# A two-layer hybrid trunk in split float32: small steps of mixers and cross attention between pieces of projections, final norm by tile

## The chip, the cores and the metric

The kernel runs on one core of one Trainium2 chip. The metric is device time in microseconds (us) of one execution, the median of the runs. PE is TensorE, DVE is VectorE, ACT is ScalarE, POOL is GpSimd, SP is SyncE, whose queue brings in the weights.

## What is computed

Two layers over x, 256 tokens of 1024 columns, in float32. In each layer:

```python
h = rms_norm(x, norm_mix[layer])
(aq, ak, av, bq, bk, bv, iq, ik, iw, cq, ckv, kr, gate_logits) = jnp.split(
    h @ w_in[layer], split_points, axis=-1)
o_a = window_gqa_sinks(...)      # 8 heads, window of 128, sinks, T5 bias
o_b = dsa_attention(...)         # token index scores, top 64 keys, 8 heads
o_c = mla_attention(...)         # low-rank q and kv, rotary keys, 8 heads
gates = jax.nn.sigmoid(gate_logits)            # three times 1024
merged = (gates[:, :, 0] * (o_a @ w_branch[layer, 0])
          + gates[:, :, 1] * (o_b @ w_branch[layer, 1])
          + gates[:, :, 2] * (o_c @ w_branch[layer, 2]))
x = x + merged @ w_out[layer]
hx = rms_norm(x, norm_xa[layer])
hm = rms_norm(mem, norm_mem[layer])
x = x + memory_cross_attention(hx, hm, xa_wq[layer], xa_wkv[layer], xa_wo[layer])
hf = rms_norm(x, norm_ffn[layer])
if layer % 2 == 0:
    x = x + swiglu(hf, ffn_w_gu[layer // 2], ffn_w_down[layer // 2])
else:
    x = x + moe_swiglu(...)      # router, 2 of 8 experts a token
```

and `rms_norm(x, final_norm)` at the end.

## The kernel before

**Weights.** All weights come from memory in units of 1 MB, by SP, into six slots of `raw`. A unit is cut into two pieces of up to 1024 columns. ACT copies a piece rounded into `whi` (L458), DVE subtracts that from `raw` and writes the rest into `wlo` (L461), both in the short float form `fp32r` that PE multiplies fast. `linear` multiplies each piece three times, high by high (L1500), activation low by weight high (L1506), activation high by weight low (L1514): 12 matmuls of up to 512 columns. There are four slots of pieces: the high half of piece p may be written once PE has used piece p - 4 (`piece_used`). The class `Splitter` does the splits in program order on ACT and on DVE; `through(l, name, b, ahead)` splits all up to the end of a block and `ahead` pieces more, `feed(n, ...)` splits n further ones. So ACT and DVE mostly have three or four pieces ready when they turn to other work.

**Blocks.** A layer has these projections, two blocks of up to 512 columns each: PA, PB, PC (inputs of the mixers A, B and C), GA, GB, GC (their gates), UQ and UKV (C's second projections), YA, YB, YC (the branches), WO (output), then XK, XQ, XV, XO (cross attention). The results of a block are in banks `lin_bank` = 2 * (number % 2) + t for the two tiles t of 128 tokens, so banks 0 to 3 alternate between blocks, and the small steps use banks 4 to 7. t = 0 sees 128 keys, t = 1 sees 256.

**Small steps.** `turn` transposes four 128-column stretches into a bank (L1527). TA, TB, TC, TQK, TM, TMEM, T2, TX, T3 are such transposes for q and k of each mixer, the merged branches, the memory and the norms. `scores` (L1549) multiplies q by k; DVE adds a bias and takes the maximum (L1845, L1848, L1855), ACT makes exponentials (L1296), DVE the inverse of the sum (L1873), POOL normalises (`normalise`, L1160). `attend` then turns the probabilities into `pT` and weighs v with them (L1568). B in addition has index products (L1624), ReLU on ACT, `index_scores` on DVE (L1934), the top-k (L1948 and L1950, eight rounds for 64 keys) and a mask that POOL adds (L1218).

**What sets the order.** It is written out by hand, one program for each engine; each engine works its list from the top, and waits on semaphores in it. On PE, each small step stands between two whole blocks, `attend` for both tiles in a row. All mixers share the two score tiles `sm` and one `pT`.

**Behind cross attention.** T3 transposes the sum x times the gain for the channel mixer. In layer 0 `dense_pe` first fills banks 4 to 7 by eight float32 matmuls with a cleared `scatter` (L644), then starts the first gate and up columns (L607, L608, L612). In layer 1 the router's weights are read by POOL once XO's last block has been added, DVE makes `r_lo`, PE multiplies the router (L1743), ACT and DVE rank the experts, tokens are gathered (L737), and a loop of eight trips runs the experts (`mixer_pe`, L785, L786, L791). A second pass, `experts2`, runs only if an expert has more than 128 tokens; the flag `more` says so, and here it does not run.

**The end.** Each engine reads `more`, branches, drains; then ACT squares x (`norm_sums`, L1262), DVE takes the mean (L1790), POOL the power (L1139), DVE multiplies (L1800), SP stores 1 MB (L1118).

Of the kernel before, what the change touches and what calls it, by code (L numbers as in the profile page):

```python
# [267 lines left out]
def trunk(nc, a, out, consts, onehot, known):  # L268
    with ExitStack() as ctx:
# [22 lines left out]
        h = place("h", [P, NT, D])  # L292
        biasA = place("biasA", [P, A_H, S])
# [15 lines left out]
        sm = [place("sm0", [P, 8, P], offset=region), place("sm1", [P, 8, S], offset=region + 4 * K1)]  # L309
        qC = place("qC", [P, NT, C_H, C_QK], offset=region)  # L310
        kC = place("kC", [P, NT, C_H, C_QK], offset=region + 6 * K1)
        pT = place("pT", [P, 2, 8, P], offset=region + 12 * K1)
# [19 lines left out]
        bias_vec = place("bias_vec", [16, 384], offset=region + 4 * K1)  # L332
        bias_rows = place("bias_rows", [P, 16, S], offset=region + 22 * K1)
# [78 lines left out]
        x_settled = sem("x_settled")  # L412

# [29 lines left out]
        class Splitter:  # L443
# [26 lines left out]

            def through(self, l, name, b, ahead=0):

                self.to(min(blocks[(l, name, b)].end + ahead, self.limit(l)))

# [24 lines left out]
        STAT_COLS = {"mix": (0, 2), "lora": (6, 4), "mem": (18, 2), "xa": (24, 2), "ffn": (30, 2), "fin": (72, 2)}  # L499
# [4 lines left out]

        def nkey(l, name):
            return ("fin",) if name == "fin" else (l, name)
# [17 lines left out]
        def prob_jobs(t, nk):  # L524
            return [(4 + 2 * kt + g, pT[:, kt, 4 * g:4 * g + 4, :], heads(bank[4 + 2 * kt + g][:, :], 4))
                    for kt in range(nk // P) for g in range(2)]
# [11 lines left out]
        def TQK(l):  # L538
            return [(4 + i % 4, (qCT, kCT)[i // 4][0:C_QK, 4 * (i % 2):4 * (i % 2) + 4, i // 2 % 2 * P:(i // 2 % 2 + 1) * P],
                     heads(bank[4 + i % 4][0:C_QK, :], 4)) for i in range(8)]  # L540

        def TX(l):
            return [(4 + i % 4, (kXT, qXT)[i // 4][:, 4 * (i % 2):4 * (i % 2) + 4, i // 2 % 2 * P:(i // 2 % 2 + 1) * P],
                     heads(bank[4 + i % 4][:, :], 4)) for i in range(8)]
# [45 lines left out]
        U0, P0 = segments[0][:2]  # L590

        def dense_pe(pe):
# [9 lines left out]
            def piece(p, jobs):  # L602

                pe.wait_ge(high_ready, at("high", p))
                for hi, lo, c, b, st, en in jobs:
                    wh = whi[:, p % PIECE_SLOTS, 512 * c:512 * c + 512]
                    pe.matmul(bank[b][:, :], hi, wh, start=st, stop=False)  # L607
# [286 lines left out]
        def mixer_dve(dve, sp_, g):  # L894
# [83 lines left out]
            for t in range(NT):  # L978
                for nb in range(2):
                    dve.wait_ge(dve_freed[BACK[t][nb]], at(g, "added", "last", t, nb))  # L980
# [1198 lines left out]
```

## Time and profile before

| | us |
|---|---|
| median of three runs (2127.85 to 2128.90) | 2128.64 |
| the profiled execution by its own time | 2129.88 |
| its span in the profile | 2128.1 |
| PE busy | 1996.1 (94%) |
| DVE busy | 1551.8 (73%) |
| ACT busy | 1298.4 (61%) |
| POOL busy | 106.7 (5%) |
| mean granted clock of PE | 0.973 |
| moved from and to memory | 513 MB, 241 GB/s |

An engine is busy while one of its instructions executes. The idle time of an engine that is not the bottleneck costs nothing; idle time of PE here nearly always does. The granted clock is the share of TensorE's full speed (2.4 GHz) that was granted, 0.5 being the lower of its levels, 1.2 GHz. A row of the trace in time has the start, the duration, engine, line, operation, tiles (out<-in), number of alike instructions in a row, and in brackets the idle time before it with what ended it.

### The profile page before, as it was taken

To read this page: it belongs to the slowest core of one execution; us is meant where nothing else is said; L and a number is where in the kernel's file an instruction comes from. 1 tells how busy PE (TensorE), PEld (TensorE's weight loads), DVE (VectorE), ACT (ScalarE), POOL (GpSimd) and SP (SyncE) were. 2 spreads that over 40 slices of the span, in tenths; PEclk is the share of its full clock that TensorE was granted. 3 is DMA by queue.
4 is the path that set the end of the run, shared out by engine and by line. 5 is a ranking of instruction groups with operands and counts; after the bars stand their busy time and mean duration, and the time that the engine had idled before them with its cause. 6 is when DMAs were issued, how large, how long until landed. Compare 5 with 4: busy or idle time off the path is not lost.

```text
span 2128.1 us, 28182 instructions
## 1 busy us (share of the span) xinstructions
PE 1996.1 (94%) x9438; PEld 1643.2 (77%) x9438; DVE 1551.8 (73%) x1749; ACT 1298.4 (61%) x1655; POOL 106.7 (5%) x101
## 2 busy tenths in 40 slices
PE   7898899899998899889969999999999999999996
PEld 5776778778887777678748888888888888888885
DVE  4676675444545667666449989898998989899896
ACT  4455553444444545544437778787777878778784
POOL 1122100100000104100000000000000000000000
PEclk9999999999999999999979999999999999999999
DMA  8343455255554334355319999999999999999993
GB/s 267 112 168 115 142 167 160 98 192 193 184 178 137 128 112 142 123 178 173 115 63 354 375 331 375 326 359 359 349 375 325 369 331 364 355 346 377 324 370 132
DMA packets 227892, 513.04 MB, mean 241 GB/s; under 512 B 8193, under 2 KB 19265, under 8 KB 227825
## 3 DMA queue, kind: packets, MB, share of 16 engines
q1 hardware_dynamic: 223568, 502.51, 66.8%
q0 software_dynamic: 2160, 7.52, 1.3%
q10 hardware_dynamic: 2096, 2.12, 0.3%
q8 instruction: 41, 0.67, 0.1%
q14 instruction: 27, 0.21, 0.0%
HBM read 511.05 MB, written 1.07 MB: 241 GB/s over the span
## 4 chain that ended last, share of the span: by engine, by line
PE 85%; DVE 7%; ACT 4%; issue 2%; DMA 1%; POOL 1%; DVEq 0%; SPq 0%; ACTq 0%; POOLq 0%
PE bank L785 14%; PE bank L791 14%; PE bank L786 14%; PE bank L1500 7%; PE bank L1506 7%; PE bank L1514 7%; PE bank L612 4%; PE bank L607 4%; PE bank L608 4%; DVE wlo L461 3%; PE bank L1527 2%; PE bank L737 2%; PE bank L753 1%; ACT whi L458 1%; PE bank L815 1%
## 5 line engine op out<-in xcount | busy, mean ns | idle before, releaser
L461 DVE TENSOR_TENSOR wlo<-raw,whi 128x1024 fp32r<-128x1024 f32 (+3 forms) x958 | 1151.5, 1236 | 321.8 <-ACT whi L458 301.0
L458 ACT ACTIVATE whi<-raw 128x1024 fp32r<-128x1024 f32 (+3 forms) x958 | 1000.5, 1056 | 455.9 <-PE bank L1514 202.7
L785 PE MATMUL bank<-whi,xg_hi 128*128 128x512 f32 x896 | 354.5, 396 | 1.8 <-ACT whi L458 1.8
L786 PE MATMUL bank<-whi,xg_lo 128*128 128x512 f32 x896 | 349.2, 390 | 0.0
L791 PE MATMUL bank<-wlo,xg_hi 128*128 128x512 f32 x896 | 276.5, 390 | 0.1
L791 PEld LDWEIGHTS bank<-wlo,xg_hi 128*128 128x128 f32 x896 | 168.1, 188 | 36.3 <-DVE wlo L461 0.5
L785 PEld LDWEIGHTS bank<-whi,xg_hi 128*128 128x128 f32 x896 | 168.3, 188 | 36.0 <-ACT whi L458 2.6
L786 PEld LDWEIGHTS bank<-whi,xg_lo 128*128 128x128 f32 x896 | 168.4, 188 | 33.3
L785 PE MATMUL bank<-whi,hidT_hi 128*128 128x512 f32 x448 | 175.1, 391 | 0.0
L786 PE MATMUL bank<-whi,hidT_lo 128*128 128x512 f32 x448 | 174.4, 389 | 0.0
L1500 PE MATMUL bank<-whi,hT_hi 128*128 128x512 f32 (+3 forms) x576 | 151.4, 388 | 2.8 <-ACT hT_hi L1275 2.8
L1506 PE MATMUL bank<-whi,hT_lo 128*128 128x512 f32 (+3 forms) x576 | 147.2, 381 | 1.1 <-DVE hT_lo L1813 1.1
L1514 PE MATMUL bank<-wlo,hT_hi 128*128 128x512 f32 (+3 forms) x576 | 145.7, 378 | 0.2
L791 PE MATMUL bank<-wlo,hidT_hi 128*128 128x512 f32 x448 | 137.9, 389 | 0.0
L1500 PEld LDWEIGHTS bank<-whi,hT_hi 128*128 128x128 f32 x576 | 106.8, 195 | 23.9 <-issue 3.6
L1506 PEld LDWEIGHTS bank<-whi,hT_lo 128*128 128x128 f32 x576 | 107.4, 194 | 20.3 <-DVE hT_lo L1813 2.0
L1514 PEld LDWEIGHTS bank<-wlo,hT_hi 128*128 128x128 f32 x576 | 106.1, 191 | 19.1 <-DVE wlo L461 1.0
L791 PEld LDWEIGHTS bank<-wlo,hidT_hi 128*128 128x128 f32 x448 | 84.1, 188 | 17.7
L786 PEld LDWEIGHTS bank<-whi,hidT_lo 128*128 128x128 f32 x448 | 84.1, 188 | 17.3
L785 PEld LDWEIGHTS bank<-whi,hidT_hi 128*128 128x128 f32 x448 | 84.1, 188 | 17.2
L607 PE MATMUL bank<-whi,hT_hi 128*128 128x512 f32 x224 | 88.1, 393 | 0.0
L608 PE MATMUL bank<-whi,hT_lo 128*128 128x512 f32 x224 | 87.2, 389 | 0.0
(286 smaller groups left out, 2169.5 us busy)
## 6 DMA issues: line engine op xcount, KB each, us to landing
raw<-in_moe_w_gu SPq DMA_DIRECT2D x224, 1024.0 KB, 6.7
raw<-in_moe_w_down SPq DMA_DIRECT2D x112, 1024.0 KB, 6.7
raw<-in_w_in SPq DMA_DIRECT2D x34, 1024.0 KB, 5.1
raw<-in_ffn_w_gu SPq DMA_DIRECT2D x28, 1024.0 KB, 5.2
raw<-in_xa_wkv SPq DMA_DIRECT2D x16, 1024.0 KB, 5.1
raw<-in_ffn_w_down SPq DMA_DIRECT2D x14, 1024.0 KB, 4.9
raw<-in_w_branch SPq DMA_DIRECT2D x12, 1024.0 KB, 5.0
raw<-in_w_out SPq DMA_DIRECT2D x8, 1024.0 KB, 5.0
```

The source lines that it names most:

```text
L458: self.eng.activation(whi[:, ps, 0:size], src, ACT.Copy).then_inc(high_ready, mark(high_ready, "high", p))
L461: self.eng.tensor_tensor(wlo[:, ps, 0:size], src, whi[:, ps, 0:size].bitcast(F32), ALU.subtract).then_inc(low_ready, mark(low_ready, "low" ...
L607: pe.matmul(bank[b][:, :], hi, wh, start=st, stop=False)
L608: pe.matmul(bank[b][:, :], lo, wh, start=False, stop=False)
L612: ins = pe.matmul(bank[b][:, :], hi, wl, start=False, stop=en)
L737: ins = pe.matmul(bank[b][:, i * P:(i + 1) * P], h[:, t, (4 * half + i) * P:(4 * half + i + 1) * P], pick[:, t], start=t == 0, stop=t == N ...
L785: pe.matmul(o, hi[:, k], wh, start=first and (c == 0 or outs[0] != outs[1]), stop=False)
L786: pe.matmul(o, lo[:, k], wh, start=False, stop=False)
L791: ins = pe.matmul(bank[outs[c]][:, :], hi[:, k_of(c)], wl, start=False, stop=en)
L1500: pe.matmul(outs[t], hi[:, k0 + kk, t * P:(t + 1) * P], whi[:, p % PIECE_SLOTS, kk * w_:(kk + 1) * w_], start=k0 + kk == 0, stop=False)
L1506: pe.matmul(outs[t], lo[:, k0 + kk, t * P:(t + 1) * P], whi[:, p % PIECE_SLOTS, kk * w_:(kk + 1) * w_], start=False, stop=False)
L1514: ins = pe.matmul(outs[t], hi[:, k, ts], wl, start=False, stop=k == blk.kt - 1)
```

## The change

Five things are changed.

1. On PE, `linear` is called with `first` and `last`, so that a block is given in parts, and the small steps stand between pieces. `attend` is cut into `turn_probs` and `weigh`. B's and C's scores come earlier: B's around YA's first piece, C's within GB's first block. TQK becomes TK and TQ, TX becomes TXK and TXQ, TM and T3 go by halves. The products and probabilities of cross attention stand between pieces of XV and XO.
2. The mixers have score tiles and probability tiles of their own (`smA`, `smB`, `smC`, `pTA`, `pTB`, `pTC`). C's mask is set by DVE (`masked_line`) in place of POOL. The squares for C's low-rank norms write into `merged` in place of `sm`.
3. On ACT and DVE the splits go by `upto(l, name, b, k)`: split up to and with piece k + 1 of that block. So one or two pieces are ahead of PE.
4. Behind XO: the squares for the norm of the channel mixer go by halves (`half_square`); in layer 0 two pieces are split before, four `fp32r` matmuls zero the banks behind the first gate and up columns; in layer 1 the router's weights are asked for at the scores of cross attention, `r_lo` is made in cross attention's second half, and the router's products go by halves into bank 0.
5. The final norm stands ahead of the branch, by tile, into tiles of its own (`y_out`), and each tile is stored by a DMA of 512 KB. POOL reads `more` before it; if the second pass runs, norm and stores are repeated in it. ACT waits for `more_known` ahead of the experts.

```diff
+            def upto(self, l, name, b, k):
+                self.to(min(blocks[(l, name, b)].piece0 + k + 2, self.limit(l)))
...
-                for t in range(NT):
-                    attend(l, "A", t, sm[t], lambda kt, par, h0: vA[:, kt, 32 * h0:32 * h0 + 64], two)
-                linear(l, "GA", 0, hT_hi, hT_lo)
+                linear(l, "GA", 0, hT_hi, hT_lo, last=2)
+                turn_probs(l, "A", 0, smA[0])
...
-                for t in range(NT):
-                    scores(l, "B", t, pair_banks(t), lambda hh: qBT[64 * (hh % 2):64 * (hh % 2) + 64, hh // 2],
-                           lambda hh: kBT[64 * (hh % 2):64 * (hh % 2) + 64])
-                linear(l, "GB", 0, hT_hi, hT_lo)
-                linear(l, "GB", 1, hT_hi, hT_lo)
...
+                scores(l, "B", 0, pair_banks(0), q_of, k_of)
...
+                linear(l, "YA", 0, oT_hi, oT_lo, last=1)
+                scores(l, "B", 1, pair_banks(1), q_of, k_of)
+                linear(l, "YA", 0, oT_hi, oT_lo, first=1)
+                linear(l, "YA", 1, oT_hi, oT_lo, last=1)
...
+                linear(l, "GB", 0, hT_hi, hT_lo, first=1, last=2)
...
+                scores(l, "C", 0, line_banks(0), q_of, k_of)
+                linear(l, "GB", 0, hT_hi, hT_lo, first=2, last=3)
+                scores(l, "C", 1, line_banks(1), q_of, k_of)
+                linear(l, "GB", 0, hT_hi, hT_lo, first=3)
...
+            gate_up("dense first", P0)
             pe.wait_ge(expert_step, at("dense", "zero"))
             for b in range(4, 8):
                 fill(pe, b, "dve")
-                pe.matmul(bank[b][:, :], scatter[:, 0], cst[:, 0:512], start=True, stop=False)
-            gate_up("dense first", P0)
+                pe.matmul(bank[b][:, :], hidT_hi[:, 0, 0], hT_hi[:, 0:2, :], start=True, stop=False)
...
                 if l:
-                    pool.wait_ge(dve_freed[lin_bank(l, "XO", 1, 1)], at("merge", l, "XO", 1, 1))
+                    pool.wait_ge(bank_full[7], at(l, "X", "S", 1, 7))
...
+            def final_squares(g):
+                for t in range(NT):
+                    act.wait_ge(dve_freed[BACK[t][0]], at(g, "added", "last", t, 0))
+                    act.wait_ge(dve_freed[BACK[t][1]], at(g, "added", "last", t, 1))
+                    square((g, "fin", "ssq", t), x[:, t, :], y_junk[:, t, :], FIN_COLS[g] + t)
+
             again = act.value_load(more[0:1, 0:1], min_val=0, max_val=1)
+            final_squares("experts")
             with tally.perhaps(), act.If(again > 0):
                 mixer_act(act, sp_, "experts2")
+                final_squares("experts2")
             act.drain()
-            act.wait_ge(x_settled, at("x_final"))
-            norm_sums(0, "fin", x, h)
```

The places on which most rests, as the instructions stand there. First PE at mixer A's probabilities, layer 0, before: behind PC's last piece, transposes of the probabilities (`sm`) and weighted sums (`pT`, `vA`) of both tiles in a row, then GA.

```order
L1527 MATMUL bank<-cst,sm_68 128x128 x8
L1568 MATMUL bank<-pT,vA 64x256 x4
L1527 MATMUL bank<-cst,sm_69 128x128 x16
L1568 MATMUL bank<-pT,vA 64x256 x8
L1500 MATMUL bank<-whi,hT_hi 128x512 x4
L1506 MATMUL bank<-whi,hT_lo 128x512 x4
L1514 MATMUL bank<-wlo,hT_hi 128x512 x4
```

The same place in the changed program, behind GA's second piece (three rows make a piece), to the first piece of GA's second block.

```order
L1631 MATMUL bank<-cst,smA_68 128x128 x8
L1604 MATMUL bank<-whi,hT_hi 128x512 x4
L1610 MATMUL bank<-whi,hT_lo 128x512 x4
L1618 MATMUL bank<-wlo,hT_hi 128x512 x4
L1674 MATMUL bank<-pTA_76,vA 64x256 x4
L1604 MATMUL bank<-whi,hT_hi 128x512 x4
L1610 MATMUL bank<-whi,hT_lo 128x512 x4
L1618 MATMUL bank<-wlo,hT_hi 128x512 x4
L1631 MATMUL bank<-cst,smA_69 128x128 x16
L1604 MATMUL bank<-whi,hT_hi 128x512 x4
L1610 MATMUL bank<-whi,hT_lo 128x512 x4
L1618 MATMUL bank<-wlo,hT_hi 128x512 x4
```

Between each transposition and its weighted sum there is now a piece of three products, and the first tile's transposition stands two pieces of GA later. The second: DVE from the last rounds of the second tile's top-k, before.

```order
L1950 MATCH_REPLACE score<-top_63,score 128x256
L1948 MAX top_63<-score 128x8
L1950 MATCH_REPLACE score<-top_63,score 128x256
L461 TENSOR_TENSOR wlo<-raw,whi 128x1024
L1954 TENSOR_SCALAR score<-score 128x256
L1880 COPY qCT<-bank 96x4x128 x2
L1880 COPY kCT<-bank 96x4x128 x2
L1901 TENSOR_TENSOR merged<-bank,gate 128x512 x2
L1848 SCALAR_TENSOR_TENSOR sm_68<-bank,biasB 128x4x128 x2
L1848 SCALAR_TENSOR_TENSOR sm_69<-bank,biasB 128x2x256 x4
L1901 TENSOR_TENSOR merged<-bank,gate 128x512 x2
```

And in the changed program, from the same rounds, with the merges of YA, the take-outs of C's k and q, and the maximum of B's first tile.

```order
L2128 MAX top_63<-score 128x8
L2130 MATCH_REPLACE score<-top_63,score 128x256
L2128 MAX top_63<-score 128x8
L2130 MATCH_REPLACE score<-top_63,score 128x256
L2134 TENSOR_SCALAR score<-score 128x256
L2081 TENSOR_TENSOR merged<-bank,gate 128x512 x2
L2056 COPY kCT<-bank 96x4x128 x2
L2031 TENSOR_REDUCE sstats<-smB_70 128x8
L2081 TENSOR_TENSOR merged<-bank,gate 128x512 x2
L470 TENSOR_TENSOR wlo<-raw,whi 128x1024
L2056 COPY qCT<-bank 96x4x128 x2
L470 TENSOR_TENSOR wlo<-raw,whi 128x1024
```

B's scaled scores have moved ahead of the top-k, whose last four rounds now have no split between them, and the take-outs of `kCT` and `qCT` have gone apart, behind the merges. The third: DVE behind the last expert, before, with the semaphores waited for.

```order
L925 TENSOR_TENSOR x<-bank,x 128x512 [waits bank7_full]
L925 TENSOR_TENSOR x<-bank,x 128x512 [waits bank2_full]
L925 TENSOR_TENSOR x<-bank,x 128x512 [waits bank3_full]
L2142 UNCONDITIONAL_BRANCH [waits bank2_freed_by_dve,bank3_freed_by_dve,bank7_freed_by_dve,bank6_freed_by_dve]
L2145 COPY sstats<-x 128x1
L1790 TENSOR_SCALAR stats<-stats 128x2 [waits squares_ready]
L1800 SCALAR_TENSOR_TENSOR h<-x,stats,gain_88 128x1024 [waits gain0_loaded,rstd_ready]
L1800 SCALAR_TENSOR_TENSOR h<-x,stats,gain_88 128x1024
```

And in the changed program.

```order
L964 TENSOR_TENSOR x<-bank,x 128x512 [waits bank7_full]
L964 TENSOR_TENSOR x<-bank,x 128x512 [waits bank2_full]
L964 TENSOR_TENSOR x<-bank,x 128x512 [waits bank3_full]
L2371 TENSOR_SCALAR stats<-stats 128x1 [waits squares_ready] x2
L2376 SCALAR_TENSOR_TENSOR y_out<-x,stats,gain_97 128x1024 [waits rstd_ready,gain0_loaded]
L2376 SCALAR_TENSOR_TENSOR y_out<-x,stats,gain_97 128x1024 [waits rstd_ready]
L2382 UNCONDITIONAL_BRANCH
```

The means and multiplications now stand ahead of the branch, each waiting for its tile's own squares or power.

## Rows read from the trace of the kernel before

**Rows 1.** The page: busy time of each engine, and the chain that ended last by engine.

```profile
PE 1996.1 (94%) x9438; PEld 1643.2 (77%) x9438; DVE 1551.8 (73%) x1749; ACT 1298.4 (61%) x1655; POOL 106.7 (5%) x101
...
PE 85%; DVE 7%; ACT 4%; issue 2%; DMA 1%; POOL 1%; DVEq 0%; SPq 0%; ACTq 0%; POOLq 0%
```

**Rows 2.** Stretches; start:end, length, busy us (instructions) by engine, granted clock, DMA.

```profile
46.50:418.60 372.10, 338.76 (x1712) 282.06 (x1711) 229.34 (x315) 176.13 (x316) 48.31 (x41) 0.95 0.42 140
418.60:429.90 11.30, 6.92 (x25) 3.70 (x24) 9.63 (x14) 8.14 (x12) 2.41 (x4) 0.85 0.24 57
...
694.90:1071.00 376.10, 339.74 (x1712) 284.50 (x1711) 229.81 (x316) 179.26 (x321) 47.23 (x39) 0.95 0.41 138
1071.00:1109.00 38.00, 19.16 (x92) 14.61 (x90) 16.51 (x58) 9.63 (x17) 2.82 (x4) 0.69 0.06 15
1109.00:2109.00 1000.00, 999.20 (x4591) 820.55 (x4589) 908.08 (x881) 790.08 (x831) 0.00 (x0) 1.00 0.95 346
2109.00:2128.10 19.10, 3.67 (x8) 1.44 (x8) 5.78 (x10) 2.19 (x4) 0.71 (x1) 0.73 0.15 58
```

**Rows 3.** Waits of PE, 46.5 to 418.6; line, releaser: us, times, longest.

```profile
PE bank L1568 <- ACT pT L1309: 5.3, 3, 3.6
PE bank L1624 <- DVE score L1934: 5.0, 1, 5.0
...
PE bank L1527 <- DVE merged L1907: 3.1, 2, 2.9
```

**Rows 4.** PE in time; start, us, line, operation, count, idle before and releaser.

```profile
89.76 4.36 PE L1624 MATMUL bank<-kiT 32*128 32x256 f32 x16 [5.01 <-DVE score L1934]
...
277.16 2.06 PE L1500 MATMUL bank<-whi,hT_hi 128*128 128x512 f32 x4
...
284.79 1.07 PE L1500 MATMUL bank<-whi,hT_hi 128*128 128x512 f32 x4
...
287.51 1.07 PE L1500 MATMUL bank<-whi,hT_hi 128*128 128x512 f32 x4
```

**Rows 5.** Groups of DVE and ACT, 46.5 to 418.6; busy us, mean ns, idle before.

```profile
L461 DVE TENSOR_TENSOR wlo<-raw,whi 128x1024 fp32r<-128x1024 f32 (+4 forms) x92 | 117.7, 1293 | 76.1 <-ACT whi L458 75.7
...
L458 ACT ACTIVATE whi<-raw 128x1024 fp32r<-128x1024 f32 (+4 forms) x91 | 93.4, 1037 | 92.7 <-PE bank L1514 92.6
```

**Rows 6.** Groups of DVE around the second top-k, 150 to 172, by form.

```profile
L1948 DVE MAX8 top<-score 128x8 f32<-128x256 f32 x8 | 3.4, 424 | 0.1
L1950 DVE MATCH_REPLACE8 score<-top,score 128x256 f32<-128x256 f32 x8 | 3.3, 409 | 0.0
```

**Rows 7.** DVE and POOL in time, around 84 and 189; columns as in 4.

```profile
84.31 4.18 DVE L461 TENSOR_TENSOR wlo<-raw,whi 128x1008 fp32r<-128x1008 f32 x2 [1.42 <-ACT whi L458]
...
189.75 4.11 DVE L461 TENSOR_TENSOR wlo<-raw,whi 128x1024 fp32r<-128x1024 f32 x1 [0.75 <-ACT whi L458]
...
83.06 3.60 POOL L1160 TENSOR_TENSOR sm<-sm,sstats 128x2048 f32<-128x2048 f32 x1 [9.02 <-DVE sstats L1873]
...
189.16 3.60 POOL L1160 TENSOR_TENSOR sm<-sm,sstats 128x2048 f32<-128x2048 f32 x1 [2.12 <-DVE sstats L1873]
```

**Rows 8.** PE in time behind XO, layer 0 and layer 1.

```profile
425.24 5.24 PE L644 MATMUL bank<-cst,scatter 128*128 128x512 f32 x8 [3.30 <-DVE scatter L2131]
...
1081.93 0.37 PE L1743 MATMUL bank<-hT_hi,r_hi 128*8 128x256 f32 x1 [7.51 <-DVE r_lo L2128]
```

**Rows 9.** All engines in time behind the last expert.

```profile
2112.80 0.69 DVE L925 TENSOR_TENSOR x<-bank,x 128x512 f32<-128x512 f32 x1 [0.17 <-PE bank L753]
...
2117.58 0.15 DVE L2145 COPY sstats<-x 128x1 f32<-128x1 f32 x1 [3.74 <-issue]
...
2120.38 0.71 POOL L1139 TENSOR_TENSOR stats<-stats 128x2 f32<-128x2 f32 x1 [1039.49 <-DVE stats L1790]
2121.12 2.48 DVE L1800 SCALAR_TENSOR_TENSOR h<-x,stats,gain 128x1024 f32<-128x1024 f32 x2 [0.90 <-POOL stats L1139]
2123.63 0.41 SPq L1118 DMA_DIRECT2D out<-h  x1
```

More of the change, by code:

```diff
@@ L607, in piece @@
                     pe.matmul(bank[b][:, :], hi, wh, start=st, stop=False)
+                if half is not None:
+                    for t in range(NT):
+                        pe.wait_ge(dve_freed[4 + 2 * t + half], at("lo", 0, "T3", t, half))
+                for hi, lo, c, b, st, en in jobs:
+                    wh = whi[:, p % PIECE_SLOTS, 512 * c:512 * c + 512]
                     pe.matmul(bank[b][:, :], lo, wh, start=False, stop=False)
@@ L1252, in _, with final_power @@
             load_gain(0, ("fin", "gain"), a["final_norm"])
-            pool.wait_ge(more_known, at("more"))
-            power(("fin",), cols(0, "fin"))
+            def final_power(g):
+                c = FIN_COLS[g]
+                for t in range(NT):
+                    pool.wait_ge(mean_ready, at(g, "fin", "ms", t))
+                    pool.tensor_tensor(stats[:, c + 4 + t:c + 5 + t], stats[:, c + 2 + t:c + 3 + t], stats[:, 95:96],
+                                       ALU.pow).then_inc(rstd_ready, mark(rstd_ready, g, "fin", "rstd", t))
+            pool.wait_ge(more_known, at("more"))
+            again = pool.value_load(more[0:1, 0:1], min_val=0, max_val=1)
+            final_power("experts")
+            with tally.perhaps(), pool.If(again > 0):
+                final_power("experts2")
+            pool.drain()
         @block.scalar
@@ L1394, in _ @@
-                sp_.through(l, "UQ", 1, 2)
+                        square((l, "lora", "ssq", 2 * t + q), tokC[:, t, o:o + w_], merged[:, t, o:o + w_], c0 + 2 * t + q)
+                sp_.upto(l, "GA", 0, 2)
+                probs_out(l, "A", 0)
+                sp_.upto(l, "GA", 0, 3)
+                weighed_high(l, "A", 0)
+                sp_.upto(l, "GA", 1, 0)
+                gates(l, "GA", 0)
+                probs_out(l, "A", 1)
+                sp_.upto(l, "GA", 1, 1)
+                weighed_high(l, "A", 1)
@@ L1518, in linear @@
                     ins.then_inc(piece_used, mark(piece_used, "used", p))
-                if last is None:
+                if last in (None, len(blk.pieces)):
                     same("lin", l, name, b, 1)
@@ L1633, in _ @@
+                weigh(l, "A", 1, v_of, two)
+                linear(l, "GA", 1, hT_hi, hT_lo, first=1, last=2)
                 for t in range(NT):
@@ new lines, in _ @@
+                linear(l, "GB", 0, hT_hi, hT_lo, last=1)
+                for i, (b, _, _) in enumerate(TQ(l)):
+                    pe.wait_ge(rope_step, at(l, f"qrope{i // 2}", "done"))
+                    turn([(qC[:, i // 2, 4 * (i % 2) + j, :], C_QK, j * P) for j in range(4)], b, ("act", "dve")[i % 2], l, "TQ", i)
+                linear(l, "GB", 0, hT_hi, hT_lo, first=1, last=2)
+                q_of = lambda hh: qCT[0:C_QK, hh]
+                k_of = lambda hh: kCT[0:C_QK, hh]
+                for i in range(4):
+                    pe.wait_ge(freed[i % 2][4 + i], at(l, "TK", i, "out"))
+                    pe.wait_ge(freed[i % 2][4 + i], at(l, "TQ", i, "out"))
```

790 lines of the change are left out of this document (476 added, 314 removed).

## The prediction, as put on record before the changed kernel was timed

> **What bounds the kernel now.** The page first: TensorE (PE) is busy for 94% of the span, and the chain that ended last lies for 85% on it [rows 1]. So a microsecond counts only where PE is idle, or runs at the lower clock. Where that is, the table by stretches tells [rows 2]. In the expert loop of layer 1 (1109 to 2109 us) PE is busy for 999.2 of 1000 us, and the change leaves that loop and most of the dense loop as they are. What can be won lies in five other places. From the A/B/C projections' second block (PB) to the end of cross attention (XO) PE is idle for 372.1 - 338.8 = 33.3 us in layer 0 and for 376.1 - 339.7 = 36.4 us in layer 1. Between XO and the dense mixer, 11.3 us; between XO and the experts, 38.0 us, at a granted clock of 0.69 of full; behind the last expert, 19.1 us with 3.67 us of PE in them.
>
> Then the waits of PE in the first of these stretches [rows 3]: always a handful of matmuls (transposes, scores, probabilities) that need something which DVE, ACT or POOL has only just got its input for. While PE stands there, nothing else is put before it. The largest is single: 5.0 us for `score`. Last, the clock. After that wait 16 small matmuls took 4.36 us; behind the 2.9 us wait for `merged` four matmuls of a piece took 2.06 us where they take 1.07 us later [rows 4]: half of full speed, 1.2 in place of 2.4 GHz. The mean granted clock of 0.95 over 372.1 us is at most 18.6 us lost; part of this lies over idle time, and from the records I take 15 us (16 in layer 1). So each layer holds 33.3 + 15 = 48 and 36.4 + 16 = 52 us that better order could give back, and no more.
>
> **The change, part by part.** *The order on PE.* Small steps now stand between pieces of a projection. A piece is 12 matmuls of 512 columns, and pieces follow one another in 2.72 us (284.79 to 287.51) [rows 4], so a result has one to four pieces (2.7 to 11 us) in which to be ready. PE's own work stays the same, but there are some 12 more changes between transposes and products, about 0.1 us each: 1.2 us. Walking the new order of all engines by durations of before, I find these waits left in a layer: 1.0 at the third piece of GA's first half (ACT does four squares ahead of its split); 0.5 before A's first weighted sum; 2.5 in GB, where DVE has the second top-k ahead of the merges which free the projections' banks: eight rounds of 0.42 + 0.41 and 0.09 us for the loading of values, 7.3 us [rows 6], two splits, 2.6, the scores before them, 2.5, and two merges, 1.4, are 13.8 us, against three pieces, 8.2, and some 3.1 of scores and transposes on PE; 2.3 before C's scores, since the take-outs of q stand behind a split whose high half waits for B's softmax on ACT; 0.3 there again; 1.4 at YB's second half, behind C's softmax; 0.5 in GC; 0.5 in WO; 0.8 at the memory's transposes; 2.0 in cross attention. Sum 11.8, with the changes 13.0 us a layer.
>
> *The splits, 1 to 2 pieces ahead in place of 3 to 4.* That is what makes the small steps early: DVE and ACT turn to them sooner. It also is the weak point. There are 92 splits in the stretch, 1.29 us each on DVE and 1.04 us on ACT [rows 5], well under the 2.72 us of a piece, so the rate is no problem; a disturbance of more than 3 us is. The trace has such ones: while POOL normalised for 3.60 us from 189.16 on, a single split on DVE took 4.11 us, from 189.75 to 193.86, and while it did so from 83.06 on, two took 4.18 us, 1.6 more than twice the mean; the second of these is what the 5.0 us wait for `score` holds [rows 3, 7]. At 189 us PE lost nothing, for three pieces were ready. In the changed kernel POOL still normalises A, B, C and X and adds B's mask, and one or two pieces are ready. Four places in a layer are open: A's second tile beside the index scores (3 us), B's mask (1), C's second tile (2.5), X (1), at most 7.5; none, if POOL's work falls beside operations that read banks. I take 5, nearer to the rows than to nothing.
>
> The Trainium skill speaks against the change here ("SBUF — State Buffer", Who interferes with whom): a DVE instruction with two SBUF inputs contends with a GpSimd one that reads SBUF, the pair is locked for the whole instruction, and the second one fully blocks. A split is such an instruction and a normalisation is too. The trace agrees in the 4.11 us beside the 3.60 us [rows 7]. By the rule alone every overlap costs up to 3.6 us, five long ones a layer 18 us; by the rows at 189 us, nothing where cover is left.
>
> *The clock.* Before, 33.3 us of waits went with 15 us at half speed, 0.45 us per us. What is left, 13 + 5 = 18 us, would by that ratio cost 8 us; but the slow records follow waits of 2.9 and 5.0 us, and what is left is mostly shorter. Between 0 and 8, I take 2.5. So 20.5 us stay in a layer. Gain: 48.3 - 20.5 = 27.8 in layer 0 and 52.2 - 20.5 = 31.7 in layer 1.
>
> *XO to the dense mixer.* Before: two turns of transposes with a wait between, then 3.30 us of waiting for a cleared tile, which stands behind the squares and the mean on DVE, then eight zeroing matmuls that took 5.24 us (float32, not the split form), all ahead of the first weights [rows 8]. Now four zeroing matmuls in the split form stand behind the first gate and up columns (about 1 us), half of x's transposes are before XO's end is evicted, and the first two pieces are split ahead. 11.3 us become some 5.3: half of the transposes and the zeroing 1.5, adding, multiplying and copying (three steps of 0.69 us on DVE [rows 9] and their hand-overs) 3, the rest, 0.8, for the hand-over to the first piece. Gain 6.0, at least 5.2.
>
> *XO to the experts.* PE waited 7.51 us for `r_lo`, whose weights were asked for only behind XO, and which stood behind the squares, the power on POOL and the scaling of x [rows 8]. The request now leaves at the scores of X, some 50 us sooner, and `r_lo` is made in the second half of cross attention. Next late is the low half of x's second transposes; with it the gain is 7.0 to 9.4 and I take 8.2. The waits behind it, for the ranks and for the gather, stay.
>
> *The end.* Before: the four additions end at 2113.5; DVE then reads a flag and branches, 3.74 us, before ACT may square; 2.8 us from there to POOL, POOL 0.71, DVE 2.48, a store of 1 MB issued at 2123.63 with 4.5 us to the end: 19.0 us [rows 9]. Now the squares of a tile start when its own two additions are over, POOL's power and the last multiplication go by tile, and 0.5 MB leaves before the last tile is done; the branch comes behind. The flag is still read by DVE behind its additions; its share of the 3.74 us isn't seen by itself, between 0 and 3.7 us, and I take 1.5. 2113.5 + 1.5 + 1.9 for means and power of the last tile + 1.24 for its multiplication + 4.5 to land = 2122.6, a gain of 5.5, of which I leave 0.3 for the second tile's squares: 5.2; 6.5 if the reading is nothing and the halved store saves 0.5, 3 if POOL's own reading of the flag holds its power up.
>
> *Costs nothing.* C's mask by DVE, two short clears next to work of PE; `lora` squares into another tile; separate buffers of probabilities; the same number of table loads.
>
> Sum: 27.8 + 31.7 + 6.0 + 8.2 + 5.2 = 78.9. The profiled execution took 2129.88 us by its own time (span 2128.1), 1.2 above the median of 2128.64. 2129.9 - 78.9 - 1.2 = 2049.8, so 2050.
>
> **The rivals.** *Cover holds.* Neither the lock nor the clock costs anything, the 13.0 us alone are left: 15 us more gain, 2035. For it: PE was never starved of a piece in 92 splits, and DVE is busy for 229 of 372 us [rows 2]. Against it: cover was thicker. With the upper ends at router and end, and half of the walked waits gone, 2022.
>
> *Stalls come in chains.* A late split delays the take-out behind it on the same engine, that one the next softmax, and so on; with waits as I walked them times 1.5 (19.5), the full 7.5 and the full ratio of the clock (8) a layer keeps 35 us: 29 us less gain, 2079; half way there, 2065. For it: ACT and DVE now have the same order of pieces and small steps, in which each is behind the other.
>
> *Slower than before.* Just-in-time splits starve PE at pieces: high half, low half and piece follow one another where they ran abreast. The whole gain of 79 us is used up if each of the 2 x 92 pieces lost 0.43 us. From rows, a high half and a low half in sequence take 1.04 + 1.29 = 2.3 us against 2.72 of a piece [rows 4, 5], so with one piece in hand nothing is lost, and it would need this in nearly all pieces. At 0.5 us each: 2142.
>
> *It does not do what it says.* The order is written by hand, and the steps stand where the text puts them; what could fail is one of the waits, so that a step stands earlier but waits as long. Then only junctions and end remain, 19.4 us: 2109.
>
> **How the numbers follow.** Forecast 2050 (2042 to 2058): 0.42. Cover holds, 2022 to 2042: 0.27. Chains, 2058 to 2085: 0.23. Waits that merely move, 2085 to 2124: 0.04. Slower: 0.03; about the same: 0.01. From 2026 to 2074 holds some 8 in 10. A difference of 0.2% (4 us) is about what a measurement of this kernel tells from none; faster by more 0.96, within it 0.01, slower by more 0.03.
>
> **What would show it.** In the profile of the changed kernel: the stretch PB to XO some 28 to 32 us shorter in each layer with PE's busy time 8 to 15 us lower (clock 0.98 or more); no wait for `score`, `merged` or `pT` above 1 us; in their place waits for `whi` and `wlo` at the successors of L458 and L461, the largest around GB and beside POOL's normalisations; DVE splits of 3 to 5 us there; XO to the dense mixer 5 us; no wait for `r_lo`; 14 us behind the last expert. I am wrong on the lock if no split is above 2 us or if long ones have no idle PE behind them; on the walk if a wait of more than 3 us stands at a place not named here; and on the kind of gain if the loops at 430 to 667 and 1109 to 2109 have changed their length.

## The result, and the profile after

The changed kernel took 2063.46 us (median of four runs, 2062.0 to 2064.88) against 2128.77 us for the kernel before in the same comparison: a ratio of 0.9686, with a 95% interval of 0.9664 to 0.9708. That is a gain of 65 us, where 79 were forecast; 2063.5 lies in the range of 2026 to 2074, but 13.5 us above the 2050 said.

The profiled span is 2062.7 us (before 2128.1). First the page, then the stretches that answer to [rows 2]: PB to XO of layer 0, XO to the first transposes of layer 1, those to PB, PB to XO of layer 1, XO to the experts, the experts, the end.

```profile
PE 1968.2 (95%) x9434; PEld 1618.3 (78%) x9434; DVE 1553.6 (75%) x1753; ACT 1291.3 (63%) x1663; POOL 110.0 (5%) x98
...
PE 88%; DVE 4%; ACT 3%; issue 2%; DMA 2%; POOL 0%; SPq 0%; DVEq 0%; ACTq 0%; POOLq 0%
```

```profile
46.40:399.30 352.90, 331.14 (x1720) 273.69 (x1718) 234.56 (x321) 176.57 (x324) 49.55 (x40) 0.97 0.44 150
399.30:645.10 245.80, 237.79 (x1076) 196.47 (x1076) 124.86 (x128) 105.15 (x120) 2.42 (x4) 1.00 0.53 179
645.10:669.50 24.40, 22.23 (x112) 19.18 (x113) 14.35 (x17) 12.14 (x17) 0.72 (x1) 0.86 0.37 121
669.50:1020.80 351.30, 328.46 (x1720) 272.02 (x1718) 231.72 (x320) 177.74 (x327) 49.48 (x39) 0.98 0.43 148
1020.80:1048.90 28.10, 15.15 (x82) 12.24 (x81) 16.06 (x58) 7.96 (x16) 1.30 (x2) 0.76 0.06 19
1048.90:2049.00 1000.10, 999.77 (x4592) 821.03 (x4592) 908.06 (x881) 790.44 (x831) 0.00 (x0) 1.00 0.95 346
2049.00:2062.70 13.70, 3.67 (x8) 1.44 (x8) 6.02 (x9) 2.43 (x5) 2.12 (x2) 0.84 0.21 82
```

PE is busy for 95% of the span in place of 94, and its chain holds 88% in place of 85 [rows 1]. Layer by layer, against the same marks in the trace of before (372.1, 253.3, 23.0, 376.1, 37.4, 1000.7 and 19.0 us), the gains are 19.2, 7.5, -1.4, 24.8, 9.3, 0.6 and 5.3 us. Both loops kept their length: the experts 1000.7 and 1000.1 us, and the dense mixer 242 us from its first product to the transposes of layer 1, the 2.7 us of T3 aside that now stand in between. The two stretches PB to XO gave 44.0 us where 59.5 had been forecast; the junctions behind XO and the end gave what was said, or more. Not forecast is the -1.4: at the start of layer 1, PE waited 1.88 us for the low half of `h` (1.10 before), and the eight matmuls from there on took 3.5 us (2.1 before).

What is left of waits in PB to XO of layer 0, to be held against [rows 3]:

```profile
PE bank L1604 <- DVE merged L2081: 8.4, 1, 8.4
PE bank L1604 <- DVE qC L2003: 4.2, 1, 4.2
PE bank L1618 <- DVE wlo L470: 4.0, 2, 2.4
PE bank L1604 <- ACT whi L467: 3.6, 4, 1.6
PE bank L1631 <- DVE hm L1975: 1.0, 2, 0.5
PE bank L1604 <- ACT hT_hi L1330: 0.6, 2, 0.3
```

`score`, `pT` and `smX` are gone. But one wait of 8.4 us for `merged` and one of 4.2 us for `qC` stand there. The first is longer than any wait of before, the second longer than all but one. The other 9.2 us are ten short waits, mostly for pieces. (What PE waits for at these rows are banks: `merged` and `qC` name the DVE step that frees them.) The two are 12.6 of 21.8 us of idle time. In time, on PE:

```profile
135.53 2.04 PE L1604 MATMUL bank<-whi,cT_hi 128*128 128x512 f32 x4 [4.22 <-DVE qC L2003]
...
168.58 2.05 PE L1604 MATMUL bank<-whi,hT_hi 128*128 128x512 f32 x4 [8.41 <-DVE merged L2081]
```

The four matmuls behind each took 2.05 us, twice their 1.07 [rows 4].

### The profile page after: what moved, and what is told of

The parts are those of the page before. It is cut to its first block, busy times and chain, and to the rows that moved or that the text cites. A ratio compares the mean times of both kernels' runs of the same rounds, so it can differ in the third digit from the quotient of the medians.

```text
span 2062.7 us, 28183 instructions
## 1 busy us (share of the span) xinstructions
PE 1968.2 (95%) x9434; PEld 1618.3 (78%) x9434; DVE 1553.6 (75%) x1753; ACT 1291.3 (63%) x1663; POOL 110.0 (5%) x98
## 3 DMA queue, kind: packets, MB, share of 16 engines
HBM read 511.05 MB, written 1.07 MB: 248 GB/s over the span
## 4 chain that ended last, share of the span: by engine, by line
PE 88%; DVE 4%; ACT 3%; issue 2%; DMA 2%; POOL 0%; SPq 0%; DVEq 0%; ACTq 0%; POOLq 0%
PE bank L824 15%; PE bank L830 15%; PE bank L825 15%; PE bank L1604 7%; PE bank L1610 7%; PE bank L1618 7%; PE bank L641 4%; PE bank L651 4%; PE bank L647 4%; PE bank L1631 2%; DVE wlo L470 2%; PE bank L776 2%; PE bank L792 2%; ACT whi L467 1%; PE bank L1653 1%
## 5 line engine op out<-in xcount | busy, mean ns | idle before, releaser
L1604 PEld LDWEIGHTS bank<-whi,hT_hi 128*128 128x128 f32 x576 | 101.7, 192 | 53.7 <-issue 26.6
L641 PE MATMUL bank<-whi,hT_hi 128*128 128x512 f32 x224 | 60.7, 393 | 2.9 <-ACT whi L467 1.7
L1330 ACT ACTIVATE hT_hi<-bank 128x512 fp32r<-128x512 f32 x40 | 21.8, 596 | 63.6 <-PE bank L1631 25.4
```

The lines of the kernel that those rows point to most:

```text
L1604: pe.matmul(outs[t], hi[:, k0 + kk, t * P:(t + 1) * P], whi[:, p % PIECE_SLOTS, kk * w_:(kk + 1) * w_], start=k0 + kk == 0, stop=False)
```

## The experiments

All times are medians of four runs, beside runs of the kernel before (medians of 2129.6 to 2130.5 us in these comparisons); the ratio is to the kernel before, with its 95% interval. To see a single layer, I give the start of the transposes T3 in the trace of layer 0, which stand in XO: 392.76 us in the changed kernel.

### What the 8.4 us are made of

DVE, ACT and POOL around this wait, in the changed kernel:

```profile
134.44 0.23 DVE L2134 TENSOR_SCALAR score<-score 128x128 f32<-128x128 f32 x1
134.59 1.01 DVE L2003 COPY qC<-bank 128x512 f32<-128x512 f32 x2
...
145.92 4.54 DVE L470 TENSOR_TENSOR wlo<-raw,whi 128x1024 fp32r<-128x1024 f32 x2
...
158.66 1.23 DVE L470 TENSOR_TENSOR wlo<-raw,whi 128x1024 fp32r<-128x1024 f32 x1 [3.84 <-ACT whi L467]
...
167.05 1.28 DVE L2081 TENSOR_TENSOR merged<-bank,gate 128x512 f32<-128x512 f32 x2
```

```profile
156.14 0.59 ACT L1364 ACTIVATE kCT<-bank 96x512 f32<-96x512 f32 x1 [10.41 <-PE bank L1631]
...
157.51 2.00 ACT L467 ACTIVATE whi<-raw 128x1024 fp32r<-128x1024 f32 x2
```

```profile
87.76 4.01 POOL L1203 TENSOR_TENSOR smA<-smA,sstats 128x2048 f32<-128x2048 f32 x1 [8.30 <-DVE sstats L2049]
...
146.06 3.32 POOL L1261 TENSOR_TENSOR smB<-smB,score 128x1024 f32<-128x1024 f32 x1 [1.26 <-DVE smB L2024]
```

Three things meet. The scores of B were late, since two splits from 145.92 on took 4.54 us beside POOL's mask of 3.32 us (two splits of 1.29 us would be 2.6). Then, inside the second top-k, DVE stood for 3.84 us before the split at 158.66: its high half was ACT's step at 157.51, and ACT had first to take out `kCT` at 156.14, which waits for the transposes of k on PE. Only behind the top-k, at 167.05, came the merges that free the banks. My sum had 13.8 us of DVE against 11.3 of PE, 2.5 us; with 3.8 and 2.1 more it is 8.4. That these three add up is argued here, not shown: the run with POOL cut short, below, takes the 2.1 away, and the wait stays at 8.4.

**The second top-k without splits in it.** The two splits come behind the first merges.

```diff
-                    if r % 2 == 1:
+                    if r % 2 == 1 and t == 0:
                         sp_.toward(l, name, b, k)
...
                     merge(l, "YA", 0, t, True)
-                take_out(l, "TK", TK(l))
                 sp_.upto(l, "GB", 0, 0)
+                take_out(l, "TK", TK(l))
```

> The changed kernel, but DVE's second top-k runs its eight rounds without splits between them, and the two splits of GB's first block come behind YA's first merges. Theory chain (the 8.4 us wait of PE at GB holds 3.84 us in which DVE stood inside the top-k for a high half that ACT could make only behind the transposes of k, and 2.4 us of the splits themselves): the wait for merged falls from 8.4 to about 2.2 us a layer; one of about 1 to 2 us for the low half of GB's first piece appears; 3 to 5 us gain a layer, 2063.5 becomes some 2055. Rival lock (the wait is as long because POOL's mask blocked DVE's splits before the top-k): the wait falls only by the 2.4 us of the splits moved, 2060.

2068.11 us, ratio to before 0.9706 (0.969 to 0.9722): not 8 us faster than the changed kernel. Whether it is slower isn't shown, for the intervals of the two ratios overlap; its T3 stands 1.1 us later, at 393.87. The wait for `merged` is 2.33 us, just as the chain says. The rest went elsewhere. PE, then DVE:

```profile
161.79 1.47 PE L1604 MATMUL bank<-whi,hT_hi 128*128 128x512 f32 x4 [2.33 <-DVE merged L2081]
...
166.15 2.08 PE L1618 MATMUL bank<-wlo,hT_hi 128*128 128x512 f32 x4 [1.18 <-DVE wlo L470]
...
176.54 3.75 PE L1653 MATMUL bank<-kCT,qCT 96*128 96x128 f32 x16 [3.22 <-DVE qCT L2056]
```

```profile
161.45 5.78 DVE L470 TENSOR_TENSOR wlo<-raw,whi 128x1024 fp32r<-128x1024 f32 x2
```

The two splits now stand beside POOL's second mask and took 5.78 us, so PE waits for the low half (1.18) and then for `qCT` (3.22). The waits are 6.7 us in place of 8.4, but they are spread, and the clock was lower: 16 score matmuls took 3.75 us (2.02 in the run with both top-ks spread, below), and the granted clock from 155 to 186 us was 0.78, against 0.83 in the changed kernel. PE was busy for longer there, with fewer matmuls. First this run, then the changed kernel (start:end, length, PE, PEld, DVE, ACT, POOL busy, granted clock):

```profile
155.00:186.00 31.00, 24.27 (x105) 19.81 (x104) 24.87 (x37) 16.36 (x43) 6.44 (x2) 0.78 0.21 68
```

```profile
155.00:186.00 31.00, 22.59 (x113) 18.95 (x113) 22.50 (x40) 15.89 (x43) 6.46 (x2) 0.83 0.20 69
```

The theory of the chain was right on the size of the wait and wrong on the gain: here a shorter wait that is followed by two more was worth nothing.

**Only the merges ahead of the second top-k.**

```diff
-                topk(l, 1, "GB", 0, 0)
                 for t in range(NT):
                     merge(l, "YA", 0, t, True)
+                topk(l, 1, "GB", 0, 0)
```

> The changed kernel, but YA's two first merges stand ahead of the second top-k on DVE. Theory chain: the wait for merged is gone, but the take-outs of C's k stand behind the same top-k, so PE waits for them some 6 us at C's q transposes one piece later: gain 1 to 3 us a layer at most, 2059 to 2063. Rival (only the banks of the projections were missing): 8.4 us and 2.6 us of low clock a layer are won, 2042.

2062.61 us, 0.9682 (0.9666 to 0.9698): no difference from the changed kernel that the intervals allow to call one; in the trace T3 stands 2.7 us earlier, at 390.09. The wait for `merged` is gone, and another takes its place one piece later:

```profile
167.25 2.77 PE L1631 MATMUL bank<-cst,qC 128*96 128x128 f32 x12 [4.53 <-DVE kCT L2056]
...
175.80 2.02 PE L1653 MATMUL bank<-kCT,qCT 96*128 96x128 f32 x16 [1.64 <-DVE qCT L2056]
```

This speaks for the chain: the banks were not the only thing that stood behind the top-k.

**Both top-ks earlier, spread over gaps of DVE.** DVE stood idle for 3.06 us at 98.8 and for 2.69 us at 113.5 in the changed kernel. The first top-k's rounds go there, the second's between UQ and B's second scores, with no splits inside.

```diff
-            def topk(l, t, name, b, k):
+            def topk(l, t, r0, r1):
...
                 evac(l, "PC", 1, 1, lambda b: [(tokC[:, 1, 336:672], b[:, 0:336], 1.0)])
+                topk(l, 0, 0, 4)
...
                 sp_.upto(l, "GA", 1, 1)
+                topk(l, 0, 4, 8)
                 weighed_low(l, "A", 1)
...
-                topk(l, 0, "UKV", 0, 0)
+                topk(l, 1, 0, 3)
                 sp_.upto(l, "UKV", 0, 0)
...
                 sp_.upto(l, "YA", 0, 0)
+                topk(l, 1, 3, 5)
...
                 scaled_scores(l, "B", 0, pair_banks(0), smB[0], biasB, HD ** -0.5)
+                topk(l, 1, 5, 8)
```

> The changed kernel, but the rounds of both top-ks stand earlier on DVE, in gaps that the trace shows: the first one's in GA, the second one's between UQ and B's second scores, with no split inside. Theory chain: the waits of 8.4 us for merged and of 4.2 us for C's q are gone, and the half clock behind them (2.6 and 2.3 us): up to 17 us a layer, less new waits of some 4: 2035 to 2042. Rival (these waits pass to the next small step, since ACT and POOL are as late): less than half of it, 2050 or above.

2035.24 us, 0.9552 (0.9536 to 0.9568): 28 us below the changed kernel, 95 below before. T3 stands at 379.67, 13.1 us earlier in one layer. Both waits are gone and nothing as long has come for them. The longest are these two, and the granted clock from 155 to 186 us is 1.00 in place of 0.83:

```profile
98.41 1.19 PE L1618 MATMUL bank<-wlo,hT_hi 128*128 128x512 f32 x4 [2.42 <-DVE wlo L470]
...
165.38 2.02 PE L1653 MATMUL bank<-kCT,qCT 96*128 96x128 f32 x16 [2.64 <-DVE qCT L2056]
```

```profile
155.00:186.00 31.00, 28.36 (x154) 23.26 (x153) 23.19 (x29) 20.07 (x49) 5.54 (x3) 1.00 0.32 102
```

Up to just behind the start of T3, first the changed kernel, then this run:

```profile
46.40:393.29 346.89, 325.19 (x1693) 269.03 (x1692) 232.28 (x318) 175.83 (x323) 49.55 (x40) 0.97 0.43 147
```

```profile
46.40:380.20 333.80, 321.45 (x1693) 266.58 (x1692) 231.83 (x318) 175.66 (x323) 47.17 (x40) 0.99 0.46 152
```

So the place of the two top-ks (and of the splits within them) cost 14 us a layer. In layer 0, of 13.1 us, 9.4 are idle time of PE (21.7 became 12.3: the two waits of 12.6 us went, 3.3 us of new ones came), and 3.7 us are busy time for the same 1693 matmuls, which is what the clock gave back. The rival, that the wait passes on, is false for this one.

### How thin the cover is

**One more piece ahead, everywhere.**

```diff
-                self.to(min(blocks[(l, name, b)].piece0 + k + 2, self.limit(l)))
+                self.to(min(blocks[(l, name, b)].piece0 + k + 3, self.limit(l)))
```

(and the same in `toward`)

> The changed kernel with one more piece split ahead everywhere between PB and XO. If the thin cover is what costs (my prediction: 5 us a layer of lock, and the slower rival), the waits for high and low halves, 7.6 us in layer 0, fall to under 3: 4 us or more a layer won, about 2055. If the place of the top-k costs, these two waits (8.4 and 4.2 us) stay or grow by the extra splits ahead of small steps, and the sum is within 4 us of 2063.5 or above it.

2064.17 us, 0.969 (0.9673 to 0.9706): as the changed kernel. The waits for high and low halves, 7.6 us in layer 0, have nearly gone (0.28 us is left), so cover does what it is for. In their place PE waits for probabilities before their weighted sum, 5.34 us, and a little more for `qC`; the 8.39 us for `merged` are as they were:

```profile
107.02 1.97 PE L1674 MATMUL bank<-pTA,vA 128*64 128x256 f32 x8 [5.34 <-issue]
...
173.39 2.04 PE L1604 MATMUL bank<-whi,hT_hi 128*128 128x512 f32 x4 [8.39 <-DVE merged L2081]
```

A small step that stands behind one more split is later by that split and by what it waits for. In this order of steps one piece more came out even, so the number of pieces ahead was not the lever; with the top-ks moved it was not tried.

### POOL beside DVE

**POOL's large operations cut to one column of each head.** The rest of the probabilities stays unnormalised and unmasked, so the router sends tokens another way, the second pass over the experts runs, and the whole time (3072.08 us) tells nothing; layer 0 up to XO does.

```diff
+                v = v[:, :, 0:1]
                 pool.tensor_tensor(v, v, sstats[:, MIX[m], t, 3, 0:n_heads].unsqueeze(2).to_broadcast([P, n_heads, v.shape[2]]),
...
-                    v = smB[t][:, :, 0:NK[t]]
+                    v = smB[t][:, :, 0:1]
...
```

> The changed kernel, but POOL normalises and masks only one key column of each head (the rest of the probabilities stays unnormalised and unmasked, so the time alone is of use). Theory of the lock: DVE splits above 2 us disappear; the waits for the low half of 2.44 and 1.52 us a layer are gone, and 2.1 of the 8.4 us at GB; with the clock 5 to 7 us a layer, 2050 to 2054. Rival (the lock falls beside covered work, the rest is the order): within 2 us of 2063.5.

T3 stands at 386.52, 6.2 us earlier, and no split in it is above 1.42 us. The waits for low halves, 2.4 and 1.5 us, are gone, and 1.3 us for a high half has come; PE idles for 2.7 us less, and the other 3.5 us are shorter busy time, at a higher clock. Of the wait for `merged` I had expected 2.1 us to go, and it is as long as it was:

```profile
98.12 1.20 PE L1605 MATMUL bank<-whi,hT_hi 128*128 128x512 f32 x4 [1.32 <-ACT whi L467]
...
165.22 2.04 PE L1605 MATMUL bank<-whi,hT_hi 128*128 128x512 f32 x4 [8.39 <-DVE merged L2082]
```

When DVE was not held up, it reached the same split inside the top-k sooner and stood longer for ACT: the chain through the transposes of k set that moment, and the lock there cost nothing by itself. This run can't tell the lock from the mere length of POOL's operations, since both went; the next one can.

**One exchange on DVE.** The inverse for A's second tile, which lets POOL start its normalisation, comes behind two splits. Nothing is left out.

```diff
                 index_scores(l, 0)
-                inverse(l, "A", 1, 8, True)
                 sp_.upto(l, "PC", 1, 2)
+                inverse(l, "A", 1, 8, True)
                 index_scores(l, 1)
```

> The changed kernel with one pair of steps on DVE exchanged: the inverse for A's second tile comes behind PC's splits, so POOL's 4.0 us normalisation falls beside index scores, which read a bank, and no longer beside two splits. Nothing is left out. Theory of the lock (POOL's reads block a DVE operation with two SBUF inputs): the splits at that place take 1.2 us each or less, not 5.35 together, the 2.44 us wait of PE for the low half and the 0.3 to 1.4 us behind it are gone: 2 to 4 us a layer, 2056 to 2060. Rival (DVE's list is simply too long there): under 1 us a layer.

2057.99 us, 0.966 (0.9643 to 0.9676): 5.5 us below the changed kernel, 2.7 a layer. The intervals of the two ratios still touch; in the trace T3 stands at 389.73, 3.0 us earlier. The pair of splits, first in the changed kernel, then here, and under it POOL's normalisation here, beside index scores that read a bank:

```profile
87.50 5.35 DVE L470 TENSOR_TENSOR wlo<-raw,whi 128x672 fp32r<-128x672 f32 x2
```

```profile
87.31 2.00 DVE L470 TENSOR_TENSOR wlo<-raw,whi 128x672 fp32r<-128x672 f32 x2
```

```profile
89.79 3.60 POOL L1203 TENSOR_TENSOR smA<-smA,sstats 128x2048 f32<-128x2048 f32 x1 [10.21 <-DVE sstats L2049]
```

5.35 us have become 2.00, and the normalisation went from 4.01 us (87.76, above) to 3.60 us. That settles the lock: it is the overlap, not the length of DVE's list, which is the same. Of the 3.0 us in layer 0, 1.3 are idle time (the waits of 2.44 and 0.29 us went, one of 1.33 us came), the rest shorter busy time. The Trainium skill ("SBUF — State Buffer", Who interferes with whom) says that `tensor_tensor` with both inputs in SBUF contends with GpSimd's reads; the trace agrees, and also in that the index scores, whose other input is a bank, ran at their pace (seven in 3.60 us with and without).

### How far single exchanges go

**Five exchanges on top of the spread top-ks**: this inverse; the take-outs of C's q ahead of a split and of B's softmax; YB's second block split ahead of C's softmax; two more pieces of XO, and one more of the dense mixer, ahead.

```diff
+                take_out(l, "TQ", TQ(l))
+                sp_.upto(l, "GB", 0, 1)
                 softmax(l, "B", 0, 8, P, smB[0])
-                sp_.upto(l, "GB", 0, 1)
-                take_out(l, "TQ", TQ(l))
...
-                softmax(l, "C", 0, 8, P, smC[0])
                 sp_.upto(l, "YB", 1, 0)
+                softmax(l, "C", 0, 8, P, smC[0])
...
+                sp_.upto(l, "XO", 0, 2)
...
-                    sp_.dense(P0, 2)
+                    sp_.dense(P0, 3)
```

> The kernel with both top-ks spread (2035.2 us) and five more exchanges: inverse of A's second tile behind PC's splits; take-outs of C's q ahead of a split and of B's softmax; YB's second block split ahead of C's softmax; two more pieces of XO and one more of the dense mixer split ahead. Gone should be the waits of 2.4 and 0.9 us in GA, 2.6 at C's scores, 1.25 in YB, 1.6 at XO in each layer, 1.7 at the dense mixer: up to 19 us, of which passing on takes a third: 2020 to 2026. If each wait only hands over to the next engine: 2032 or above.

2028.93 us, 0.9522 (0.9507 to 0.9538): 6.3 us, not 9 to 15. The waits named went, but for 1.33 us in GA and the one at C's scores. There a split stands behind B's softmax on ACT, and DVE stood 4.2 us for its high half before it could scale C's first scores. One new wait, and behind it 16 matmuls in 6.87 us that take 3.62 in the changed kernel:

```profile
165.32 6.87 PE L1654 MATMUL bank<-kCT,qCT 96*128 96x256 f32 x16 [3.54 <-DVE smC L2022]
```

**Two more**: C's first scores scaled ahead of that split and maximum, and two pieces of GA split ahead of C's squares on ACT.

```diff
+                sp_.upto(l, "GA", 0, 1)
                 c0, _ = cols(l, "lora")
...
+                scaled_scores(l, "C", 0, line_banks(0), smC[0], None, C_QK ** -0.5)
+                masked_line(l, 0)
                 sp_.upto(l, "GB", 0, 2)
                 dve.wait_ge(masked, at(l, "masked", 1))
                 masked_max(l, "B", 1, 8, S, smB[1])
                 inverse(l, "B", 0, 8)
-                scaled_scores(l, "C", 0, line_banks(0), smC[0], None, C_QK ** -0.5)
-                masked_line(l, 0)
```

> The kernel before this one (2028.9 us) with two more exchanges: C's first scores are scaled on DVE ahead of the split and of the maximum that waited for ACT's softmax of B, and two pieces of GA's first block are split on ACT ahead of C's squares. The one long wait left in each layer's mixers, 3.5 us for smC with 4.5 us of half clock behind it, should go, and 1.3 us in GA: up to 18 us in both layers; 2014 to 2019 if it is the order of single steps that decides, 2025 or more if the softmax of B has become the chain and only shows at another step.

2022.48 us, 0.9492 (0.9476 to 0.9508), the fastest kernel of this study: 108 us below the kernel before and 41 below the changed one. It lies between the two forecasts: 6.5 us gained, with 1.67 us of the wait left one step on. Layer 0 from PB on, with T3 at 371.89:

```profile
46.40:380.00 333.60, 325.21 (x1722) 269.57 (x1722) 235.27 (x324) 178.97 (x328) 47.59 (x40) 1.00 0.47 159
```

The granted clock is 1.00 over 333.6 us, and PE idles for 8.4 us of them.

## Why the prediction was right, and where it was off

The direction, the bounding engine and the range were right; the time fell into the band that I had given to chains of stalls (2058 to 2085), not into that of the forecast (2042 to 2058). Two of the signs that I had named speak against me: PB to XO became 19 and 25 us shorter, not 28 to 32, and a wait of more than 3 us (4.2 at UKV) stands at a place that I hadn't named. In layer 0, 29.1 us stayed where I had left 20.5. Two waits hold 12.6 us of it, where my walk had 2.5 in GB; all other idle time is 9.2 us, where I had 9.3 of walked waits and 5 for the lock; the clock holds some 6, where I had 2.5. So two errors of 10 and 4 us were in part hidden by one of 5 the other way, and the range owes something to that luck. No run takes one of the five parts of the change out alone; what each gave is read from its stretch. Step by step:

- **Small steps between pieces** (right). The waits for `score`, `pT`, `smX` and `merged` of TM are gone from PE.
- **The walk** (the step that failed). I had 2.5 us at GB; it is 8.4. I summed DVE's own durations and forgot that a split inside the top-k also waits for ACT, and ACT for PE's transposes: 3.84 us. The 4.2 us at UKV I did not list at all: the eviction of UQ stands behind the first top-k, whose end (134.44) sets it. The experiment with spread top-ks shows that these two places cost 14 us a layer, 28 in all, where the two layers missed by 15.5. Three of the smaller ones were about right in place and size: 1.4 said and 1.24 found in YB, 0.8 and 1.0 at the memory's transposes, 2.0 and 1.85 in cross attention. In GA, 1.0 was said and 0.29 found (1.3 once the lock is away). Those before A's weighted sum and C's scores were not seen; that PE came there late itself is likely, for 2.64 us stand before C's scores once the top-ks are moved.
- **The lock** (the mechanism right, the size in part by luck). 3 us of waits were said for A's second tile, and the exchange gave 3.0 in layer 0, but only 1.3 of it as idle time; the rest came from the clock, which I had priced apart. For B's mask 1 us was said, and it cost no wait; for C's second tile 2.5, and the wait of 1.52 us went with POOL cut short. 5 in all said, 6.2 measured with POOL cut short, 2.7 of it idle time.
- **The clock** (mis-sized). 2.5 us said. The two pieces behind the long waits alone took 4.9 us (135.53 to 140.45) and 5.3 us (168.58 to 173.84) for 2.7 each: 4.8 us a layer. Up to T3, PE was busy for 325.2 us in the changed kernel and for 318.9 us in the fastest one, with 1693 matmuls in both and a granted clock of 1.00 in the latter: some 6 us. The term hung on the assumption that what is left would be short waits, and that short waits go without half speed. The trace of before speaks against that: from 200 to 250 us no wait of PE was above 1.6 us, and the granted clock was 0.93.

```profile
200.00:250.00 50.00, 45.12 (x195) 35.11 (x196) 30.83 (x33) 23.59 (x51) 6.55 (x4) 0.93 0.36 115
```

- **XO to the dense mixer, XO to the experts, the end**: 6.0, 8.2 and 5.2 said; 7.5, 9.3 and 5.3 measured, where the 7.5 are taken up to the end of the dense mixer. The end came out by errors that cancel: the additions end at 2053.95, and DVE read the flag in about a quarter of a microsecond, where I had 1.5; the second tile's squares (its mean comes at 2055.2) and POOL's second power (1.54 us) took what that left:

```profile
2054.20 0.15 DVE L2371 TENSOR_SCALAR stats<-stats 128x1 f32<-128x1 f32 x1 [0.24 <-issue]
...
2057.04 1.28 DVE L2376 SCALAR_TENSOR_TENSOR y_out<-x,stats,gain 128x1024 f32<-128x1024 f32 x1 [0.45 <-POOL stats L1296]
```

- **Just-in-time splits** (the rival on the slower side). It fell: PE waits for high and low halves for 7.6 us in layer 0, in six waits, and with one piece more ahead the time is the same.
- **Cover holds / chains**: the second was nearer. 2063.5 lies in its band, but not for waits 1.5 times as long everywhere: one was far too small and one was missing, and the rest were about as said or shorter.

## What to carry to other kernels

When each engine's program is written by hand, walk the new order with what each step waits for, not with durations alone: a long run of steps on one engine (here eight rounds of top-k) is stretched by all the time that a single step inside it waits for another engine. Put such runs into idle stretches that a trace shows, and let nothing that frees a bank stand behind them. And judge an exchange by the time, not by the wait that it removes: of the eight runs here, three shortened or removed the waits they were made for and gained nothing that the intervals show.

## What was not expected of the hardware

Two splits on DVE took 5.35 us beside a 4.01 us normalisation on POOL, and 2.00 us beside none: the loss (3.4 us) is nearly the whole of POOL's operation. One by one, the records look like turns that are taken, not like a shared pace. The first split (87.50 to 88.31) was at work when the normalisation began at 87.76; that one took 0.41 us more than the 3.60 of the other order and ended at 91.77. The second split began at 88.23 and ended 1.09 us behind that, where a split of its size takes 1.22 us:

```profile
88.23 4.63 DVE L470 TENSOR_TENSOR wlo<-raw,whi 128x1024 fp32r<-128x1024 f32 x1
```

TensorE ran at half speed (1.2 in place of 2.4 GHz) for the piece behind waits of 4.2 and 8.4 us, and for 16 matmuls behind one of 3.5 us (6.87 in place of 3.62 us), but not for the 16 matmuls behind one of 2.6 us (2.02 us, granted clock 1.00). The length of the wait alone doesn't tell it, though. Behind the wait of 2.4 us for a low half, in GA, the granted clock from 96 to 107 us was 0.84 in the changed kernel, 0.69 in the run with spread top-ks, and 1.00 in the run with the merges first, in this order:

```profile
96.00:107.00 11.00, 8.32 (x36) 6.04 (x37) 7.13 (x12) 6.01 (x14) 1.75 (x1) 0.84 0.29 93
```

```profile
96.00:107.00 11.00, 7.66 (x24) 5.75 (x24) 9.52 (x23) 5.25 (x12) 1.65 (x1) 0.69 0.27 85
```

```profile
96.00:107.00 11.00, 7.09 (x37) 5.11 (x37) 7.28 (x13) 6.03 (x14) 1.59 (x1) 1.00 0.26 88
```

In one comparison, waits of 2.3, 1.2 and 3.2 us in a row gave a lower mean clock over 31 us (0.78) than one of 8.4 us did (0.83). What decides between these cases stays open.
